# A mixture-of-experts block on one core: rows gathered by scaled f32 products in place of three bf16 parts, and a quarter of a down chunk loaded ahead

## The reference, cut to what matters

```python
x = x + token_mix(rmsnorm(x, norm_mix_w), ...)
x = x + cross_attend(rmsnorm(x, norm_xa_w), rmsnorm(mem, norm_mem_w), ...)
h2 = rmsnorm(x, norm_moe_w)                      # 256 x 1024
logits = h2 @ w_router + b_router
top_v, top_i = top_k(logits, 4); gates = softmax(top_v)
# for the rows xb that chose expert e:
gu = xb @ w_gate_up[e] + b_gate_up[e]
gate, up = min(gu[:, :1024], 7), clip(gu[:, 1024:], -7, 7)
y[rows] += gates * (((up + 1) * gate * sigmoid(1.702 * gate)) @ w_down[e] + b_down[e])
out = rmsnorm(x + y, norm_final_w)
```

## Time and profile before

| | us |
|---|---|
| median of 3 runs | 1185.22 (1184.13 to 1185.9) |
| the profiled execution | 1184.76 |
| its span in the profile | 1183.0 |
| TensorE busy (products) | 1134.4 |
| VectorE, ScalarE, GpSimd busy | 381.3, 181.8, 22.0 |
| weights and other data moved | 444.24 MB, mean 376 GB/s |

### The profile page before, as it was taken

One profiled execution on the slowest core, in us unless ns is written; L12 is line 12 of the kernel. 1 busy time (PEld: TensorE's weight loads), 2 busy tenths in 40 slices (PEclk: granted clock), 3 DMA queues, 4 the chain that ended last, 5 costly groups with the idle time before them and its releaser, 6 DMA issues.

```text
span 1183.0 us, 18703 instructions
## 1 busy us (share of the span) xinstructions
PE 1134.4 (96%) x7502; PEld 574.9 (49%) x7503; DVE 381.3 (32%) x891; ACT 181.8 (15%) x395; POOL 22.0 (2%) x65
## 2 busy tenths in 40 slices
PE   9999999999999999999999999999999999999996
PEld 8989889855434444344333333333333333333332
DVE  4988878455221111222211111111111111111112
ACT  4611521343100000000000000000000000000002
POOL 4000010000000000000000000000000000000000
PEclk9999999999999999999999999999999999999999
DMA  9954204989999999999999999999999999999995
GB/s 324 369 172 144 73 10 155 346 330 398 417 428 432 429 431 431 429 433 431 433 430 433 431 430 433 431 431 433 431 433 430 432 432 431 432 432 423 426 424 226
DMA packets 41353, 444.24 MB, mean 376 GB/s; under 512 B 4270, under 2 KB 5656, under 8 KB 24540
## 3 DMA queue, kind: packets, MB, share of 16 engines
q1 hardware_dynamic: 39868, 440.45, 88.9%
q0 software_dynamic: 480, 1.85, 0.6%
q10 hardware_dynamic: 960, 1.31, 0.4%
HBM read 442.55 MB, written 1.05 MB: 375 GB/s over the span
## 4 chain that ended last, share of the span: by engine, by line
PE 67%; DMA 31%; DVE 1%; ACT 0%; SPq 0%; issue 0%; DVEq 0%; ACTq 0%
DMA ring<-in_w_gate_up 30%; PE bank L1180 23%; PE bank L1171 13%; PE bank L736 7%; PE bank L732 4%; PE bank L1210 4%; PE bank L1225 3%; PE bank L875 1%; PE bank L715 1%; PE bank L1107 1%; PE bank L1296 1%; PE bank L1201 1%; PE bank L1287 1%; PE bank L913 1%; PE bank L1019 1%; PE bank L1141 1%
## 5 line engine op out<-in xcount | busy, mean ns | idle before, releaser
L1180 PE MATMUL bank<-ring,region 128*64 128x512 f32 x2048 | 464.0, 608 | 36.0 <-DMA ring<-in_w_gate_up 36.0
L1180 PEld LDWEIGHTS bank<-ring,region 128*64 128x64 f32 x2048 | 147.0, 140 | 333.5 <-issue 268.7
L1171 PE MATMUL bank<-ring,region 128*64 128x512 f32 x1024 | 226.8, 595 | 0.3 <-ACT region L1419 0.3
L2328 DVE TENSOR_SCALAR region<-bank 128x512 f32<-128x512 f32 x32 | 22.1, 691 | 573.9 <-PE bank L1180 573.9
L1171 PEld LDWEIGHTS bank<-ring,region 128*64 128x64 f32 x1024 | 71.1, 137 | 130.1 <-issue 127.2
L1419 ACT ACTIVATE region<-bank 128x256 f32<-128x256 f32 (+1 forms) x130 | 53.4, 437 | 367.0 <-PE bank L1171 251.1
L1419 ACT ACTIVATE bank<-region 128x512 f32<-128x512 f32 x32 | 19.2, 601 | 452.5 <-DVE region L2328 452.5
L736 PE MATMUL bank<-ring 128*128 128x256 f32 x392 | 86.6, 380 | 0.0
L736 PEld LDWEIGHTS bank<-ring 128*128 128x128 f32 x392 | 73.8, 190 | 10.9 <-issue 0.7
L1210 PE MATMUL bank<-region 64*128 64x512 f32 x264 | 65.6, 615 | 0.1
L1225 PEld LDWEIGHTS bank<-region,r_levels 128*128 128x128 bf16 x1536 | 61.3, 118 | 1.6 <-issue 1.6
(11 more groups left out here) (318 smaller groups left out, 774.0 us busy)
## 6 DMA issues: line engine op xcount, KB each, us to landing
ring<-in_w_gate_up SPq DMA_DIRECT2D x48, 4096.0 KB, 30.2
ring<-in_w_down SPq DMA_DIRECT2D x24, 4096.0 KB, 36.5
ring<-in_w_gate_up SPq DMA_DIRECT2D x26, 2048.0 KB, 14.3
ring<-in_w_down SPq DMA_DIRECT2D x10, 2048.0 KB, 13.3
ring<-in_w_in SPq DMA_DIRECT2D x6, 2048.0 KB, 19.8
ring<-in_w_gate_up SPq DMA_DIRECT2D x11, 1024.0 KB, 35.6
ring<-in_w_xkv SPq DMA_DIRECT2D x4, 2048.0 KB, 11.0
ring<-in_w_down SPq DMA_DIRECT2D x7, 1024.0 KB, 8.3
```

What stands on the lines that cost most here:

```text
L1171: last = pe.matmul(bk[half * ROWS:(half + 1) * ROWS, :], lhs, w[:, half * 512:(half + 1) * 512], start=start, stop=stop, skip_group_check= ...
L1180: last = pe.matmul(rows, lhs, columns[:, half], start=start, stop=stop, skip_group_check=True)
L2328: v.tensor_scalar(g_t, bank_g[:, :], LIMIT, None, ALU.min).then_inc(sem["g_clamped"], 1)
```

## The change

The rows are stored once, in f32 and in the order in which the gather takes them: `h2[p, t, k, i]`, so that each stationary tile is contiguous. The three bf16 parts, their 15 casts on ScalarE and 10 subtractions on VectorE are gone. The gather multiplies `h2` by `scaled_sel` itself, in f32, 16 products a block, and what lands in PSUM is ready; `take_rows` copies it. The selection `sel`, the scale products, `row_scales` and their semaphores are gone. `h2` takes 16 KB a partition; 4 of the 8 KB that come free are `spare`, into which SyncE loads the first quarter of chunk (1, 5), and TensorE reads it there. The last quarter of (1, 4) is loaded earlier. The gate bias of expert 0 moves ahead of the second half's gather.

```diff
+SPARE = (1, CHUNKS - 1)
-        left_over = region10[:, D:2 * D]
-        half_squares = r_t[:, 2 * D + HALF:3 * D]
+        half_squares = region10[:, D:D + HALF]
-        h2_parts = r_t[:, :].bitcast(BF16).rearrange("p (i t n) -> p i t n", i=3, t=NT)
+        h2 = r_t[:, 0:NT * D].rearrange("p (t k i) -> p t k i", t=NT, i=P)
+        spare = r_t[:, 2 * D:3 * D]
...
             load_cols(1, 3, 0, D)
+            sp.wait_ge(sem["x1_squared"], NT)
+            sp.dma_start(spare, source(*SPARE)[:, 0:D]).then_inc(sem["spare_in"], 16)
             wait_full(sp, "xo01")
             load_chunk(1, 1)
+            sp.wait_ge(sem["x2_squared"], 3)
+            load_cols(1, 4, 3 * D, SLOT)
             sp.wait_ge(sem["seeded"], NT)
             load_cols(1, 4, 0, D)
...
             load_cols(1, 4, D, 3 * D)
-            sp.wait_ge(sem["cut_ready"], CUTS * len(PIECES))
-            load_cols(1, 4, 3 * D, SLOT)
...
-                    load_cols(e, k, 0, SLOT // 2)
+                    load_cols(e, k, D if (e, k) == SPARE else 0, SLOT // 2)
...
             def gather_half(tiles, t):
                 for k in tiles:
-                    for i in range(3):
-                        last = pe.matmul(bank_a[:, k * ROWS:(k + 1) * ROWS], h2_parts[:, i, t, rows_of(k)], sel[:, t, :],
-                                         start=(t == 0 and k == 0 and i == 0), stop=(t == NT - 1 and i == 2), skip_group_check=True)
+                    last = pe.matmul(bank_a[:, k * ROWS:(k + 1) * ROWS], h2[:, t, k, :], scaled_sel[:, t, :],
+                                     start=(t == 0 and k == 0), stop=(t == NT - 1), skip_group_check=True)
...
             def gather(tiles):
                 for k in tiles:
-                    for i in range(3):
-                        for t in range(NT):
-                            last = pe.matmul(bank_a[:, k * ROWS:(k + 1) * ROWS], h2_parts[:, i, t, rows_of(k)], sel[:, t, :],
-                                             start=(i == 0 and t == 0), stop=(i == 2 and t == NT - 1), skip_group_check=True)
+                    for t in range(NT):
+                        last = pe.matmul(bank_a[:, k * ROWS:(k + 1) * ROWS], h2[:, t, k, :], scaled_sel[:, t, :],
+                                         start=(t == 0), stop=(t == NT - 1), skip_group_check=True)
...
-            keep_warm()
-            scales([0])
-
-            pe.wait_ge(sem["sel_ready"], 1)
-            pe.wait_ge(sem["cut_ready"], 3 * CUTS)
-            gather_half(range(KT // 2), 1)
+            bias_of(bank_g, 0)
+
             pe.wait_ge(sem["scaled_ready"], 1)
-            scales([1]).then_inc(sem["rs_psum"], 1)
+            pe.wait_ge(sem["xw_ready"], 3)
+            gather_half(range(KT // 2), 1).then_inc(sem["lead_rows"], 1)
...
-            pe.wait_ge(sem["rs_ready"], 1)
-            bias_of(bank_g, 0)
...
                     if not final:
-                        next_rows(1)
-                        pe.wait_ge(sem["actT_rest"], w1)
-                        pe.wait_ge(sem["scaled_ready"], pe.snap(w1 + 1))
-                        scales().then_inc(sem["xb_psum"], 1)
+                        next_rows(1).then_inc(sem["xb_psum"], 1)
...
+                            w = wk[:, a * D:(a + 1) * D]
+                            if in_spare and (j, a) == (DOWN_CHUNKS - 1, 0):
+                                pe.wait_ge(sem["spare_in"], 16)
+                                w = spare
...
-            for i in range(CUTS):
-                cut(0, i)
...
-            def scale_xb(lo, hi, signal):
+            def take_rows(lo, hi, signal):
                 src = bank_a[:, lo * ROWS:hi * ROWS].rearrange("p (k r) -> p k r", r=ROWS)
-                v.tensor_tensor(xbT[:, lo:hi, :], src, row_scales.unsqueeze(1).broadcast_to([P, hi - lo, ROWS]),
-                                ALU.mult).then_inc(signal, 1)
+                v.tensor_copy(xbT[:, lo:hi, :], src).then_inc(signal, 1)
             def weigh_rows(piece):
                 t, first, last = PIECES[piece]
-                v.tensor_tensor(left_over[:, first:last], x_res[:, t, first:last], norm_row[:, first:last],
-                                ALU.mult).then_inc(sem["xw_ready"], 1)
+                c0, rows = first // HALF * ROWS_PER, slice(first % HALF // ROWS_PER, (last - 1) % HALF // ROWS_PER + 1)
+                by_tile = h2[:, t, c0:c0 + ROWS_PER, rows].rearrange("p a i -> p i a")
+                x, w = (m[:, first:last].rearrange("p (i a) -> p i a", a=ROWS_PER) for m in (x_res[:, t], norm_row))
+                v.tensor_tensor(by_tile, x, w, ALU.mult).then_inc(sem["xw_ready"], 1)
```

More of the change, by code:

```diff
@@ L1184, in bias_of @@
                 pair_of_inner(bk, one_hot, b_gu[:, c0:c0 + D], True, False)
-            def keep_warm():
-                pe.matmul(bank_g[:, 0:T], ident[:, :], iota, start=True, stop=True)
             def gather_half(tiles, t):
                 for k in tiles:
-                    for i in range(3):
-                        last = pe.matmul(bank_a[:, k * ROWS:(k + 1) * ROWS], h2_parts[:, i, t, rows_of(k)], sel[:, t, :],
-                                         start=(t == 0 and k == 0 and i == 0), stop=(t == NT - 1 and i == 2), skip_group_check=True)
[L1196 to L1201, removed]
+                    last = pe.matmul(bank_a[:, k * ROWS:(k + 1) * ROWS], h2[:, t, k, :], scaled_sel[:, t, :],
+                                     start=(t == 0 and k == 0), stop=(t == NT - 1), skip_group_check=True)
                 return last
@@ L1268, in one_time, with expert @@
                 pe.matmul(first_of_psum, first_col, spans, start=True, stop=True).then_inc(sem["blocks_psum"], 1)
-            def expert(e, slots, counts, last_tiles={}, lead=False, final=False, by_halves=False):
+            def expert(e, slots, counts, last_tiles={}, lead=False, final=False, by_halves=False, in_spare=False):
                 def next_rows(half):
-                    pe.wait_ge(sem["sel_ready"], pe.snap(w1 + 1))
-                    gather(range(half * KT // 2, (half + 1) * KT // 2))
+                    pe.wait_ge(sem["scaled_ready"], pe.snap(w1 + 1))
+                    return gather(range(half * KT // 2, (half + 1) * KT // 2))
                 def scatter_and_combine():
@@ L1282, in scatter_and_combine @@
                         pe.wait_ge(sem["gT_ready"], 1)
-                    scatter()
+                    last = scatter()
+                    if final:
+                        last.then_inc(sem["xb_psum"], 1)
                     pe.wait_ge(sem["selg_ready"], w1)
@@ L1380, in expert @@
                                 pe.wait_ge(sem["actT_rest"], w1)
-                            last = pair(bank_d, actT[:, f, :], wk[:, a * D:(a + 1) * D], (j, a) == (0, 0),
+                            w = wk[:, a * D:(a + 1) * D]
+                            if in_spare and (j, a) == (DOWN_CHUNKS - 1, 0):
+                                pe.wait_ge(sem["spare_in"], 16)
+                                w = spare
+                            last = pair(bank_d, actT[:, f, :], w, (j, a) == (0, 0),
                                         (j, a) == (DOWN_CHUNKS - 1, DOWN_ROWS - 1))
@@ L1385, in expert @@
                         last.then_inc(sem["chunk_used"], 1)
[L1386 to L1389, removed]
+                    if not final:
                         pe.wait_ge(sem["one_hot_ready"], pe.snap(w1 + 1))
@@ L1401, in _ @@
             for e in range(HEAD):
-                expert(e, slots(e), counts(e), lead=(e == 0), by_halves=(e < BY_HALVES))
+                expert(e, slots(e), counts(e), lead=(e == 0), by_halves=(e < BY_HALVES), in_spare=(e == SPARE[0]))
             with pe.Fori(0, TURNS) as i:
@@ L1662, in gate_exps @@
                 fn(gate_ex[:, t, :], logits[:, t, :], ACT.Exp, bias=ngmax[:, t:t + 1]).then_inc(sem["gate_exps"], 1)
[L1664 to L1671, removed]
             def seed(t, half, job):
@@ L1679, in _ @@
             act.wait_ge(sem["gu_part_ready"], 3)
-            for i in range(CUTS):
-                cut(0, i)
             half_squared(0, 1)
-            for i in range(CUTS):
-                cut(1, i)
             half_squared(1, 0)
[L1686 to L1689, removed]
             seed(0, 0, "xo01")
             seed(0, 1, "eT01")
+            gate_exps(0)
             wait_taken(act, "router0")
@@ L2358, in _ @@
             weigh_rows(0)
-            rest(0, 0)
-            rest(0, 1)
             add_rows("xo", 0, 1)
@@ L2368, in _ @@
             link(newton_steps(rstd[:, 6:7], mean))
-            rest(1, 0)
             take_e(0, 1)
-            rest(1, 1)
             add_rows("xo", 1, 0)
@@ L2375, in _ @@
             choose(0)
-            rest(2, 0)
             take_e(1, 0)
-            rest(2, 1)
             def add_quarter(job, piece):
@@ L2387, in _ @@
             add_quarter("xo11a", 3)
-            dve.wait_ge(sem["cut_ready"], 2 * CUTS)
             weigh_rows(3)
             gate_weights(0)
-            rest(3, 0)
```

(14 more changed lines are left out.)

37 lines of the change are left out of this document (6 added, 31 removed).

## The result

| | before | changed |
|---|---|---|
| median of 4 runs, us | 1185.01 (1184.13 to 1185.9) | 1202.17 (1201.33 to 1203.11) |
| span of the profiled execution | 1183.0 | 1201.2 |
| mean granted TensorE clock | 0.986 | 0.993 |
| TensorE busy, us | 1134.4 | 1168.7 |
| VectorE, ScalarE busy, us | 381.3, 181.8 | 360.1, 173.8 |

What follows compares the result with a forecast made beforehand. The weight stream was taken to bound the middle, its loads needing slots that TensorE frees, and TensorE the end. Stream 5.4 us plus end 3.2 gave 8.6, so 1193.8 us against 1185.22, range 1187.5 to 1198.

Steps and rivals of the forecast that it cites:

- its side: Whole kernel: the change makes it slower, chance 0.87, against 0.09 for same and 0.04 for faster.
- its size: Whole kernel: 8.6 us slower, 1193.8 us against 1185.22.
- The price of a product: Gather on TensorE: 0.112 us per f32 instruction, two instructions a product, bounds 0.109 and 0.1425.
- Block: Each block's gather on TensorE: 32 f32 instructions, 3.58 us in place of 2.15, +1.43 us, period 27.55.
- The tail: TensorE after its last wait for weights: expert 30's gather +1.43 and expert 31's half gathers +1.75, together +3.2 us.
- The early loads: Weight stream before (1,5): 2.9 us ahead from the spare quarter and (1,4), lost at (2,0), leaving nothing at the end.
- The tightest load: Wide load (5,2), waiting for expert 3's down product: slack 1.15 us, stream 5.4 us late, carried to the end.
- At 410.5: Load issued at 410.5 us: slack 4.65, lateness 3.3, adds nothing; after it the stream is saturated.
- The clock: Start of the experts: no term for a clock fall; first weight product 0.3 us late, slots freed 0.8 late.
- A: Weight slots: slack larger than read, queue never dry, only 3.2 us at the end counts; about 1187 us, chance 0.11.
- B: Gather: each f32 instruction costs 0.1425 us, as in groups of four; +15.4 us, 1200.6, chance 0.10.
- C: Gather: f32 products priced by 64 moving columns, 0.04 us like bf16; -2.2 us, 1183.0, chance 0.05.

Runs made afterwards that it cites:

- experiment 5: Kernel before with each block's scale products done four times in blocks 0 to 30; 1194.72 us, ratio 1.0081.
- experiment 4: Early loads taken back, from the changed kernel (1197.4 us) and from that kernel with the up bias and a 256-column product ahead of the first gather (1198.76 us).
- after_again: Changed kernel run again with no edit; median 1200.88 us, runs 1196.71, 1198.83, 1202.94 and 1203.4, the profiled one 1196.71.
- experiments 5 and 6: The second of these: kernel before with four-fold scale products in blocks of experts 0 to 4 alone (1190.43 us), or in all others alone (1187.45 us).
- experiment 1: Changed kernel with the up bias and one product of 256 f32 columns moved ahead of the first half gather; 1197.85 us, ratio 1.0105.
- experiment 2: Changed kernel with two products of 256 f32 columns behind the rank products, where the kernel before had one; 1203.28 us.
- warm_early: The kernel of experiment 1: changed kernel with up bias and one 256-column f32 product ahead of the first half gather; 1197.85 us.
- no_last_gather: warm_early without the two half gathers inside expert 31; 1194.54 us.
- no_early: Changed kernel without the quarter loaded into freed memory and with the last quarter of (1, 4) loaded behind its middle as before; 1197.4 us.
- warm_late: The kernel of experiment 2: changed kernel with two products of 256 f32 columns behind the rank products; 1203.28 us.

## Why the prediction was right in its side and wrong in its size

**The price of a product: right.** 0.112 us taken, 0.108 measured; the lower bound (0.109) was the better, and the upper, from the groups of four, was a start and not a rate (experiment 5's 12 more took 1.34 us a block, 0.112 each). The rule of the Trainium skill ("TensorE: Matmul & The Clock Gate", Weight-path perf modes), that 128-column f32 weights have no fast load, agrees with 0.108 against 0.033 us. Block +1.35 for +1.43.

**The tail: right.** +3.2 forecast. It reads from the same products, the scatter in expert 30's block, to the end of the span, first in the kernel before, then in the changed one:

```profile
1132.68 1.92 PE bank L1210 x8
```

```profile
1147.69 1.92 PE bank L1199 x8
```

1183.0 - 1132.68 = 50.3 us and 1201.2 - 1147.69 = 53.5 us: 3.2 more. What changed besides is that TensorE's unbroken stretch now begins two blocks earlier; from the wait that ends at 1070.75 in the kernel before and at 1085.49 in the changed one it is 112.25 and 115.7 us, 3.45 more, but the first of these still holds a wait for weights.

**The early loads: right.** Forecast to leave nothing, and experiment 4 found less than 1 us.

**The tightest load: the mechanism right, the place wrong.** The load (5, 2) itself behaved as forecast: in after_again, counted from the same L1141 run, it was issued 6.4 us late (forecast 6.5), and the load that the kernel before issues at 436.6 landed 4.8 late (462.4 against 457.8), for 5.4. The step that failed is the next one: "At 410.5: 0.8 + 5 x 1.43 - 4.65 = 3.3, less, so that no longer adds. From there the stream is saturated and carries 5.4 us to the end". I had followed the loads to 410.5 and taken the slack to grow by 3 us an expert. It doesn't grow evenly: SyncE waits for the release of expert 8's first pair from 443.96 to 462.8 in the kernel before, and the slack there is small again, behind seven gathers. In after_again this load was issued 10.5 us late, and the last weights landed 8.7 us late (1178.0 against 1169.5, from a start 0.2 sooner), where the forecast had 5.4; with the fall of the clock they landed 12.8 us late (1184.3, from a start 1.9 later).

Read by that load the term is 1.0 + 7 x 1.35 - 1.3 = 9.2 us instead of 5.4 (the slack from experiments 5 and 6: 7 x 1.34 = 9.4 us of late release lost 8.1, and 5 x 1.34 = 6.7 lost 5.6, so 1.3 and 1.1; the landings' 3.2 is more, because the stream also lost time in starting again: expert 8's second pair landed 11.0 us behind the first in the changed kernel, 9.5 in the kernel before, 1.5 more, which leaves 1.7). With the tail that is 12.6, and the runs without the fall lie at 1196.7 to 1198.8, 12 to 14 above the kernel before.

**The clock: not seen at all.** I had costed the start's products at 2.4 GHz, a term at nothing without a reason. The start became 5.1 us late instead of 1.0; experiment 1 gave 4.3 back. The removal of keep_warm is not what brought it: the fall comes near 277.4 us, before its place, and came in experiment 2 by the mean clocks with two such products there. 12.6 + 4.1 = 16.7 of the 17.2 us measured. The traces add up more closely: for after_again 8.7 (last weights) + 3.4 (tail) - 0.2 (start) = 11.9 of 1196.71 - 1184.76 = 11.95 us, and for the changed kernel's profiled run 12.8 + 3.45 + 1.9 (start) = 18.15 of 18.15. It took both errors to leave the range: 1193.8 + 3.8 (9.2 for 5.4) = 1197.6 and 1193.8 + 4.1 = 1197.9 would each have lain just inside it. No rival named either.

**Rivals.** A (slack hides the releases) fell with experiment 5, though its premise, a 2 MB load alone faster than 8.6 us, was true (7.2). B (0.1425 a product) gave a time close to the measured one for a reason that the block's period refutes. C fell with the price.

That the fall of the clock comes from the run of narrow f32 products is supported by where it stands and by experiment 1's trace, and not more. Of the four profiled kernels with experiment 1's order two had no fall (warm_early, no_last_gather) and two a short one. By the mean clocks (0.992 to 0.994 with the long one) warm_early and no_early had no long fall in four runs each, the changed kernel had it in six of eight, warm_late in three of four, so the loads taken out of no_early may have only shifted the stretch in time. What decides it in one execution was not settled. None of the versions tried is faster than the kernel before.

## What to carry to other kernels

When a stream of transfers waits for slots that an engine frees, follow every load until the queue's backlog is truly large, the last one before saturation included, and multiply a longer block by the number of blocks ahead of the tightest one: here 1.35 us a block cost 8 to 9 us, though TensorE had 3 us to spare in each. Bytes loaded ahead help only if the next slot comes free in time. And where TensorE leaves dense work for narrow products and short waits, look at the granted clock before costing them at full speed.

## What the runs showed of the hardware

- A product with a 128x128 f32 stationary tile and 64 moving columns took two instructions of 0.108 us in runs of 16, about the same as with 32 columns (L1124, 16 instructions in 262.38 to 264.08 of the kernel before, 0.106) or 128 (0.112); a bf16 one took 0.033.
- A stretch of some 3 us with f32 products of 32 and 64 moving columns, TensorE busy by the profile but for 0.2 us (3.73 of 3.90 and 2.30 of 2.30), ended at 1.2 GHz in some executions; busy time alone did not keep the clock at 2.4. The profiled executions of the changed kernel with and without the fall are 6.2 us apart; 4.1 of it arise between L1141 and chunk 1, 2.1 stand already ahead of L1141.
- A 2 MB load into an all but empty queue landed after 7.2 us and a 4 MB load after 12.3; the 8.6 us for 2 MB taken from one row of the kernel before was no lower bound.
